# GpSimd splits u in 16-bit halves ahead of time, and transposing DMAs fetch them

## The reference

```python
def peer_mixer(x2, w_q, sub_keys, u, v):       # u, v: (16384, 1024)
    q = (xt @ w_q).reshape(T, PEER_HEADS, 2, PEER_QDIM // 2)
    s = jnp.einsum('thpd,hpkd->thpk', q, sub_keys)
    ...                                         # top 16 of 128 twice, top 16 of their sums: idx, g
    h = jnp.einsum('td,ted->te', xc, jnp.take(u, ic, axis=0))
    a = jax.nn.gelu(h, approximate=False) * gc
    return jnp.einsum('te,ted->td', a, jnp.take(v, ic, axis=0))
```

## Time and profile before

| | |
|---|---|
| median of 3 runs | 3208.13 us (3206.66 to 3216.7) |
| profiled execution | 3208.9 us, span 3207.2 us |
| mean granted clock of PE | 0.953 of full speed |
| PE, PE weight load, DVE, ACT, POOL busy | 95%, 53%, 72%, 31%, 40% |
| moved by DMA | 594.91 MB, 185 GB/s over the span |

### The profile page before, as it was taken

One profiled execution on the slowest core, in us unless ns is written; L12 is line 12 of the kernel. 1 busy time (PEld: TensorE's weight loads), 2 busy tenths in 40 slices (PEclk: granted clock), 3 DMA queues, 4 the chain that ended last, 5 costly groups with the idle time before them and its releaser, 6 DMA issues. The chain is left out here.

```text
span 3207.2 us, 49336 instructions
## 1 busy us (share of the span) xinstructions
PE 3043.3 (95%) x17450; PEld 1711.2 (53%) x17450; DVE 2321.1 (72%) x4680; ACT 1004.6 (31%) x1471; POOL 1279.3 (40%) x899
## 2 busy tenths in 40 slices
PE   8898889889999699999969999999999999999999
PEld 4444645445555477777635555555555554444444
DVE  3234465438999666666558888888888888999996
ACT  4322255323343355555411222222222222222221
POOL 1021111002443212212156666666655555555662
PEclk9999567899999799999989999999999999999999
DMA  3210010121121244555488888878888888888884
GB/s 106 70 40 0 14 40 1 34 79 55 64 73 52 93 175 186 196 196 185 171 283 287 271 292 280 274 272 289 287 275 274 272 273 287 303 305 292 309 293 174
DMA packets 256174, 594.91 MB, mean 185 GB/s; under 512 B 20768, under 2 KB 127408, under 8 KB 252976
## 3 DMA queue, kind: packets, MB, share of 16 engines
q1 hardware_dynamic: 180016, 318.63, 29.3%
q0 software_dynamic: 73728, 268.47, 23.7%
q10 hardware_dynamic: 2304, 6.29, 0.6%
HBM read 513.63 MB, written 79.69 MB: 185 GB/s over the span
## 5 line engine op out<-in xcount | busy, mean ns | idle before, releaser
L238 PE MATMUL f_y<-f_v_hi,f_a_hi 128*128 128x512 f16 x1536 | 583.5, 380 | 9.5 <-DVE p_h L2212 9.5
L239 PE MATMUL f_y<-f_v_lo,f_a_hi 128*128 128x512 f16 x1536 | 583.3, 380 | 0.0
L240 PE MATMUL f_y<-f_v_hi,f_a_lo 128*128 128x512 f16 x1536 | 583.3, 380 | 0.0
L2179 POOL DMA_INDIRECT f_rows<-in_peer_u,p_row_index x256 | 355.9, 1390 | 207.0 <-DVE f_rows L2220 124.4
L2179 POOL DMA_INDIRECT f_rows<-in_peer_v,p_row_index x256 | 310.9, 1215 | 280.7 <-DVE p_h L2230 252.4
L2220 DVE SCALAR_TENSOR_TENSOR f_rows<-f_rows,p_xs 128x1024 f32<-128x1024 f32 x256 | 379.8, 1517 | 46.5 <-DMA f_rows<-in_peer_u,p_row_index 46.5
L2230 DVE SCALAR_TENSOR_TENSOR p_h<-f_rows,f_row_a,p_h 128x1024 f32<-128x1024 f32 x256 | 394.3, 1540 | 17.6 <-DMA f_rows<-in_peer_v,p_row_index 10.8
L2212 DVE SCALAR_TENSOR_TENSOR p_h<-f_y,p_h 128x512 f32<-128x512 f32 x384 | 262.9, 685 | 109.5 <-PE f_y L240 107.5
L2190 POOL TENSOR_TENSOR f_v_lo<-f_v_in,f_v_hi 128x1024 f16<-128x1024 f32 x128 | 283.6, 2216 | 145.0 <-ACT f_v_hi L2154 143.7
L238 PE MATMUL f_hid<-p_act_hi,x_u_hi 128*128 128x384 f16 x1008 | 330.5, 328 | 2.0 <-DVEq L2197 2.0
L239 PE MATMUL f_hid<-p_act_lo,x_u_hi 128*128 128x384 f16 x1008 | 330.3, 328 | 0.0
(11 more groups left out here) (311 smaller groups left out, 5461.4 us busy)
## 6 DMA issues: line engine op xcount, KB each, us to landing
f_v_in<-in_peer_v SPq DMA_DIRECT2D x128, 512.0 KB, 5.2
dense_weights<-e_stage SPq DMA_DIRECT2D x24, 2048.0 KB, 8.7
f_g_in<-dense_weights SPq DMA_DIRECT2D x32, 1536.0 KB, 15.6
x_u_in<-in_peer_u SPq DMA_DIRECT2D x64, 512.0 KB, 4.9
e_u_in<-in_peer_u SPq DMA_DIRECT2D x48, 512.0 KB, 4.1
x_gel<-early_tiles SPq DMA_DIRECT2D x64, 384.0 KB, 3.4
early_tiles<-e_gel SPq DMA_DIRECT2D x48, 384.0 KB, 2.5
a_w_in<-in_w_in SPq DMA_DIRECT2D x24, 512.0 KB, 3.8
```

The source lines that it names most:

```text
L238: pe.matmul(out, a_hi, b_hi, start=first, stop=False)
L239: pe.matmul(out, a_hi, b_lo, start=False, stop=False)
L240: return pe.matmul(out, a_lo, b_hi, start=False, stop=last)
L2179: nc.gpsimd.indirect_dma_start(out=rows[q % ROWS][:], out_offset=None, in_=table, in_offset=bass.IndirectOffsetOnAxis(ap=T.row_index[:, ti ...
```

## The change

In the stages up to `retrieve`, a `Splitter` takes u tile by tile: SP loads it, POOL scales it, casts it to float16 (hi) and subtracts (lo), and SP stores both halves in HBM as `split_u`, 128 rows of 2048 float16 for a tile. Two buffers are used for the loads and two for the halves. 40 tiles fall to `project_in` (32 behind the eight rstds of x, before the first head rstd; then one behind each second head rstd), 16 to `gla_outputs` (two behind each rstd), 40 to `diff_attention` (b // 2 behind each unit's rstd), 16 to `project_out` (two behind each) and 16 to `retrieve` (two behind each head). Each stage waits at its end for its stores. In `project_in` the buffers lie in the room of dv, and ACT waits for all stores before it fills dv; in `diff_attention` they lie in that of dq.

The hidden layers then load [d, expert] directly with a transposing DMA on SP's queue. PE's turns, ACT's and DVE's or POOL's copies of u and the PSUM bank pair u_ps are gone; the y ring of `experts` grows from 2 banks to 4. A load of u waits for the hidden matmuls that read its buffer before (formerly for the turn). Some loops are written out in place of hardware loops.

```diff
+class Splitter:
+    def load(self, sp, i):
+        if i >= 2:
+            sp.wait_ge(self.lo_done, i - 1)
+        sp.dma_start(self.u_in[i % 2], self.u_rows[self.first + i]).then_inc(self.loaded[i % 2], 16)
+
+    def store(self, sp, i):
+        sp.wait_ge(self.lo_done, i + 1)
+        sp.dma_start(self.T.u_split[self.first + i], self.halves[i % 2].rearrange("p x d -> p (x d)")).then_inc(
+            self.stored[i % 2], 16)
+
+    def transfers(self, sp, i):
+        self.store(sp, i)
+        if i + 2 < self.count:
+            self.load(sp, i + 2)
+
+    def split(self, pool, i):
+        b = i % 2
+        pool.wait_ge(self.loaded[b], 16 * (i // 2 + 1))
+        if i >= 2:
+            pool.wait_ge(self.stored[b], 16 * (i // 2))
+        self.nc.gpsimd.tensor_scalar(self.u_in[b], self.u_in[b], S_U, None, ALU.mult).then_inc(self.scaled, 1)
+        pool.wait_ge(self.scaled, i + 1)
+        self.nc.gpsimd.tensor_copy(self.halves[b][:, 0], self.u_in[b]).then_inc(self.hi_done, 1)
+        pool.wait_ge(self.hi_done, i + 1)
+        self.nc.gpsimd.tensor_tensor(self.halves[b][:, 1], self.u_in[b], self.halves[b][:, 0],
+                                     ALU.subtract).then_inc(self.lo_done, 1)
...
+SPLIT_IN, SPLIT_IN_HEADS, SPLIT_GLA, SPLIT_DIFF, SPLIT_OUT, SPLIT_PEER = 32, 8, 2 * NT, 40, 2 * NT, 2 * PEER_H
...
@@ project_in, sync
             for c in range(1, len(COLS)):
                 for q in range(PIECES):
                     load_w(c, q)
+                    for i in itertools.islice(tiles, 2 if c < 5 and q else 1):
+                        U.transfers(sp, i)
...
@@ project_in, gpsimd
+            for i in range(SPLIT_IN):
+                U.split(pool, i)
+            for n in range(2 * NT):
+                pool.wait_ge(head_ss, n + 1)
...
+                if n % 2:
+                    U.split(pool, SPLIT_IN + n // 2)
...
@@ project_in, scalar
                 if name == "dv":
                     act.wait_ge(acc_free, BASE + first_result[c])
+                    U.all_stored(act)
...
@@ gla_outputs, gpsimd (project_out alike)
+                for i in range(2):
+                    U.split(pool, 2 * t + i)
...
@@ diff_attention, gpsimd
+                for i in itertools.islice(tiles, b // 2):
+                    U.split(pool, i)
...
@@ retrieve, gpsimd, at the end of each head
+                for i in range(2):
+                    U.split(pool, 2 * h + i)
...
@@ EarlyTiles
+    def load(self, sp, c, b):
+        if c:
+            sp.wait_ge(self.hid_done, BASE + 2 * ((c - 1) * self.ring + b) + 2)
+        sp.dma_start(self.u[b][:].rearrange("p x k e -> p (x k) e"), self.u_rows[c, b],
+                     transpose=True).then_inc(self.u_loaded[b], 16)
-    def turn(self, pe, c, b):
-    def split(self, act, c, b):
-    def low(self, pool, c, b):
...
@@ experts, sync
-                        sp.wait_ge(u_turned, BASE + n - 1)
-                        sp.dma_start(u_in[m % 2][:], u_v[view, m]).then_inc(u_loaded[m % 2], 16)
+                        sp.wait_ge(hid_done, BASE + n - 1)
+                        sp.dma_start(u[m % 2][:].rearrange("p x k e -> p (x k) e"), u_v[view, m],
+                                     transpose=True).then_inc(u_loaded[m % 2], 16)
...
@@ experts, tensor
-                    pe.wait_ge(y_added, BASE + YB * group_n + k - 1)
+                    pe.wait_ge(y_added, BASE + YB * group_n + k - YR + 1)
```

More of the change, by code:

```diff
@@ L336, in _ @@
                 load_x(t)
+            for i in range(2):
+                U.load(sp, i)
+            tiles = iter(range(U.count))
             for c in range(1, len(COLS)):
@@ L747, in _ @@
                                         ALU.pow).then_inc(rstd_done, 1)
+                for i in range(2):
+                    U.split(pool, 2 * t + i)
+        @block.sync
+        def _(sp):
+            for i in range(2):
+                U.load(sp, i)
+            for i in range(U.count):
+                U.transfers(sp, i)
+            U.all_stored(sp)
         @block.tensor
@@ L904, in _ @@
                 sp.dma_start(T.w_out[:, k, :], io.w_out[0, k * P:(k + 1) * P, :]).then_inc(w_out_loaded, 16)
+            sp.wait_ge(qk_turned, 2 * NT)
+            for i in range(2):
+                U.load(sp, i)
+            for i in range(U.count):
+                U.transfers(sp, i)
             sp.wait_ge(w_out_loaded, 16 * KT)
+            U.all_stored(sp)
         @block.gpsimd
@@ L911, in _ @@
             c = Chain(pool, pool_step)
-            for u in range(len(units)):
+            tiles = iter(range(U.count))
+            for u, (b, h) in enumerate(units):
                 pool.wait_ge(squared, u + 1)
@@ L1476, in step @@
                 h = 2 * hh + b
-                before = not (first and b == 0)
-                if before:
-                    E.turn(pe, h - 1, 1)
-                else:
-                    E.turn(pe, h, 0)
                 if not (last and b):
@@ L1484, in step @@
                     scores(h + 1)
[L1485 removed]
+                if not (first and b == 0):
                     E.hidden(pe, h - 1, 1, 0)
[L1487 removed]
                     E.hidden(pe, h - 1, 1, 1)
                 E.hidden(pe, h, 0, 0)
[L1490 to L1491 removed]
                 E.hidden(pe, h, 0, 1)
@@ L2058, in _ @@
             step(0, 0, first=True)
-            with sp.Fori(1, LATE) as c:
+            for c in range(1, LATE):
                 step(c, c)
```

255 lines of the change are left out of this document (82 added, 173 removed).

## The result

The changed kernel takes 3538.27 us (median of four runs, 3528.16 to 3551.2) against 3208.12: ratio 1.1021, 95% interval 1.1 to 1.1042. It was predicted to be slower, at 3262 us in a range of 3215 to 3375; it is 163 us beyond that range. The profiled execution took 3537.13 us, its span 3535.4.

What follows compares the result with a forecast made beforehand. PE was taken to bound the last stage and nearly spreading, DVE retrieval, a latency chain attention. Terms +35 +37 +72 +9 +5 -48 -57 gave +53 us on 3208.9: 3262 us, range 3215 to 3375 (forecast case alone 3215 to 3310).

Steps and rivals of the forecast that it cites:

- Spreading -48: Spreading stage: removing 48 turns (eight PE transposes each) from near-full PE saves 48 us (40 to 52).
- turns of the last stage -57: Last stage: removing 62 turns of 0.87 us from PE, plus more y banks, saves 57 us (45 to 65).
- A split at 4.5 us: POOL, per tile: scaling 1.03, cast 1.03, subtraction 2.13, semaphores 0.3 us; bounds 4.2 and 6.7 us.
- 79 us for each us: Stages with splits: total losses change by about 79 us for each us of a split's cost.
- its formula: Attention: POOL runs in order, so 39 splits and 21 rstds of 0.9 us follow one another from unit 8 to 29.
- hidden but for its end (+9): Output projection: splits fit its 11.23 us period; only two tiles and a store after the last rstd cost 9 us.
- The port: POOL and DVE's two-SBUF-input instructions take turns; raises attention from +55 to +72 us, GLA outputs from +32 to +37.
- First stage +35: First stage: w pieces on SP's queue wait behind stores that wait for POOL, 5.0 us a tile; +35 us.
- The three stalls: First stage: PE waits at about 52, 98 and 124 us because w pieces come late: 14, 5 and 14 us.
- Retrieval +5: Retrieval: only two splits and a store at the stage's end count, +5 us; w loads behind stores have slack.
- Transposed load hidden: Last stage and spreading: transposing loads of 512 KB cost DMA near a plain load's 1.55 us, so add no time.
- rival 1: DMA limits the last stage: at 5.2 us a load the step is 17.15 us, kernel 3360 us; chance 0.27.

Runs made afterwards that it cites:

- e2: The changed kernel with plain instead of transposing loads of u in all three stages (hidden layers then wrong): 3443.51 us, ratio 1.0731.
- e11: The changed kernel with POOL's scaling written as product plus sum of zero in one instruction: 3382.3 us, ratio 1.0533.
- e5: The changed kernel with POOL's split instructions on a fixed tile, SP storing a constant tile without waiting for POOL and loading no u for splits: 3473.34 us.
- e3: The changed kernel without splitting work: POOL fills two tiles with zeros, SP stores them 128 times; transposing loads stay: 3191.49 us, ratio 0.9917.
- e4: As e3, without splitting work, but with plain loads of u too: 3101.07 us, ratio 0.9664.
- e14: The same code as e12, one more execution with a profile: 3167.57 us.
- e10: The kernel before, changed for spreading only: 48 two-instruction splits in first stage, output projection and retrieval, through POOL's queue: 3210.51 us, ratio 1.0002.
- e12: The kernel before, changed for spreading only: 7 two-instruction splits in output projection, 41 inside spreading, through POOL's queue: 3168.39 us, ratio 0.9857.
- e9: e3 plus one-input POOL instructions of 128x1024 in several forms, three times each, behind the first stage's rstds; only durations read, no kernel time given.
- e6: The changed kernel with two-instruction splits (scale 1) and the splitter's loads and stores issued from POOL's own queue: 3376.33 us, ratio 1.0519.
- e7: e3 with four u buffers instead of two in the last stage, loads issued two tiles sooner: 3195.54 us median, ratio 0.9902 from the five shortest.

## Why the prediction was wrong, step by step

- **Spreading -48, turns of the last stage -57: right.** Measured -54.8, and -61 in the last stage with plain loads (e2).
- **A split at 4.5 us: the size of one term was wrong.** Cast and subtraction were right; the scaling took 2.79 us for 1.03, and 6.07 us lies inside the bound of 6.7, which the forecast's own range (3215 to 3310) didn't use. The nearest row, a select of 128x128, was another operation. By the prediction's own 79 us for each us, 1.57 us more is +124. Where rstds queue behind splits its formula holds: for attention at 6.05 us, 39 x 6.05 + 21 x 0.9 = 255 us from unit 8 to 29 (measured 256.7), a stage of 51 + 255 + 17 - 3 = 320 us (measured 322.5). The output projection was called hidden but for its end (+9): at 6.05 us POOL needs 12.9 us of its period of 11.23, the rstds recur every 13.06 us, and it lost 22.9. e11 confirms attention and projection at 4.45 us.
- **The port.** That POOL and DVE take turns was right (e11: 5.48 us for four products of 0.35). The amount was too high for the changed kernel itself, where attention comes out without it (320 against 322.5), since the slow scaling takes little part. In e11 it is there in attention (203.6 us from unit 8 to 29, where 39 x 4.45 + 19 = 192.5), and not in GLA outputs, which come out lower than the formula without it. Not priced at all: DVE's w_lo in the first stage.
- **First stage +35: the mechanism was right, the sizes and one term were not.** The three stalls came as described, and later, because a tile took 6.07 us: the prediction's own 35 us at 5.0 and 55 at 5.6, carried on to 6.07, give an estimate of 71, and up to the first head rstd the stage lost 70. "A few us of lower clock" were 17. But "the splits between the 16 head norms cost some 5 us, which a shorter wait elsewhere gives back" was wrong: they cost 24 (12.2 us a pair for 8.3), and nothing gave it back. Nor does a shorter split mend the stage. e11, at 4.45 us, had the three stalls (12.5, 11.1, 14.1 for 14, 5, 14), and still took 367.4 us for the 338 predicted, 18 of the difference between the head norms (91.7 us from the first to the last, 73.3 before).
- **Retrieval +5: the step that failed is that "the w loads queued on SP behind their stores have more than that in hand".** The stage has one w buffer, so w of head h + 2 can be asked for only behind the stores of the splits of the step before, and these stand last in POOL's step, behind products that wait for DVE. ACT waits 137.5 us for w, where it waited 67.8 in e5 and 73.4 in e3, which lost next to nothing; 33 us of the stage are the queue (e5), 22 POOL's time. The end of the stage was priced and the steady state wasn't.
- **Transposed load hidden: wrong, and rival 1 was right in kind.** It had +98 us over the forecast at 5.2 us of engine time; e2 and e4 measure 92 and 100 in the last stage. The late tiles' DMA share went from 0.84 to 1.10 at the same traffic. (1.10 x 998 - 0.84 x 904) us over some 58 tiles is 5.8 us more for each: 7.3 us a load where 1.55 was the estimate for a plain one, twice the 3.5 us at which the prediction said it would fail. That rival 1's size came out is partly luck: it took 5.2 us a load and a limit at a share of 1.0, and the runs show 7.3 us and 1.10. "4 KB rows like a plain load's" described the source, and the pieces that move are of 256 bytes. Who waits: DVE for gathered rows of u, 203.4 us between 1993 and 2986 (6.9 in e2), and PE, through DVE's a_lo and for u itself.
- The Trainium skill, Advanced Engine Details and Errata, section X-Bar Transpose (TRN2), says transposing transfers are as fast as regular ones, at 350 to 400 GB/s. The runs don't agree where other traffic runs beside them: the same bytes take the DMA share from 0.55 (e4) to 0.65 (e3) in spreading, and from 0.84 to 1.10 in the last stage. Nor do they agree with the 21 us that the prediction works out from the figure for one block in the Trainium skill, VectorE: DVE Perf Modes, section The three transpose paths: the profile has the landing of two transposing loads only, and these landed 5.3 and 6.3 us after their issue began.

All in all: +53 forecast, +88 for the last stage, +124 for the scaling, +52 for retrieval, and some 11 for the rest make +328. The rest is a balance and no cause of its own: some 29 in the first stage beyond what the size of a split explains (24 of it the head norms), 11 in the projection and 8 in the seams, less 17 in attention and 9 in GLA outputs (the port), 7 in spreading and 3 that retrieval and the scaling both count.

## What to carry to other kernels

An idle engine's time is free only where nothing waits behind the new work: on that engine, on the queue that serves it, and at a port it shares. 128 splits cost 347 us in five stages; 41 of a shorter form cost some 4 us (e14's 483 against e10's 479, but 514 in one execution of e12) inside the stage whose POOL the change itself had emptied. Where two limits lie close together, as SP's queue and POOL's order did in the first stage, removing one gives back only the distance to the other. When a transfer of another form replaces a plain one in a stage that already moves data for 82% of the time, take its dearest bound until a run shows its packets. And measure an instruction whose form no row shows before its price is multiplied by 128.

## What the runs showed of the hardware that was not expected

- POOL's tensor-scalar on 128x1024 float32: 2.8 us with one operation, 1.04 with two (e9, e11), whatever the output's type or place. The Trainium skill, GPSIMD Engine Reference, section 3.1 (Elementwise), puts a body of up to two operations at 1.03 cycles for an element, at 1.2 GHz an estimate of 0.88 us and the dispatch; the copy's 1035 ns and the two-operation form's 1044 fit that, the single product's 2802 doesn't.
- But for the first of them (1.13 us), the slow form runs beside DVE's products of two SBUF tensors; the fast forms and POOL's subtraction make them wait (1.92 against 5.48 us for four).
- A transposing load of 512 KB goes in some 2048 packets of 256 bytes. It holds SP's queue for 2.1 to 3.2 us in spreading, and in the last stage, at a DMA share of 1.10, for a median of 8.0 and up to 26 us (e5). A plain transfer issued by POOL takes 0.57 us of POOL in the median (e6).
- e7, whose DMA share is above 1 in the last stage, varies more between executions: 3160 to 3201 us in its five shortest, against 3202 to 3215 in thirteen of before. Whether the share is the cause is not shown.
